# An exact bf16 gather of the sample rows, and the last four experts written outside the loop

## What is computed

```
def moe(xf, w_router, b_router, w1, b1, w2, b2):        # N = 264 tokens, w1[e] 1024x2048, w2[e] 1024x1024
    logits = xf @ w_router + b_router
    top_v, top_e = lax.top_k(logits, TOP_K)             # TOP_K = 4 of 32
    gates = jax.nn.softmax(top_v, axis=-1)
    ...
    def run_block(args):
        e, toks, g = args
        xb = xf[toks]                                   # the gather
        h = xb @ w1[e] + b1[e]
        glu = jnp.minimum(h[:, ::2], SWIGLU_LIMIT)
        lin = jnp.clip(h[:, 1::2], -SWIGLU_LIMIT, SWIGLU_LIMIT)
        a = glu * jax.nn.sigmoid(SWIGLU_ALPHA * glu) * (lin + 1)
        return (a @ w2[e] + b2[e]) * g[:, None]
```

## Time and profile before

| | us |
|---|---|
| median of 3 runs | 1114.68 |
| lowest and highest of them | 1113.35, 1115.1 |
| the profiled execution, its own time | 1113.78 |
| span of the profiled execution | 1112.0 |
| PE busy | 1096.1 |
| DVE busy | 409.0 |
| ACT busy | 165.3 |
| POOL busy | 78.7 |
| bytes moved | 440.43 MB, mean 396 GB/s |

### The profile page before, as it was taken

One profiled execution on the slowest core, in us unless ns is written; L12 is line 12 of the kernel. 1 busy time (PEld: TensorE's weight loads), 2 busy tenths in 40 slices (PEclk: granted clock), 3 DMA queues, 4 the chain that ended last, 5 costly groups with the idle time before them and its releaser, 6 DMA issues.

```text
span 1112.0 us, 14748 instructions
## 1 busy us (share of the span) xinstructions
PE 1096.1 (99%) x5674; PEld 423.5 (38%) x5674; DVE 409.0 (37%) x881; ACT 165.3 (15%) x310; POOL 78.7 (7%) x103
## 2 busy tenths in 40 slices
PE   8999999999999999999999999999999999999998
PEld 6886433333333333333333333333333333332344
DVE  1737763333333333333333333333333333323255
ACT  1622330001000100010001000100001000100043
POOL 0847410000000000000000000000000000000000
PEclk9999999999999999999999999999999999999999
DMA  9988889999999999999999999999999999999971
GB/s 315 266 314 336 255 336 421 426 427 427 430 427 430 427 430 427 428 429 427 429 429 428 429 428 428 427 431 427 428 429 428 429 428 428 427 430 428 428 282 39
DMA packets 48723, 440.43 MB, mean 396 GB/s; under 512 B 10513, under 2 KB 13837, under 8 KB 23766
## 3 DMA queue, kind: packets, MB, share of 16 engines
q1 hardware_dynamic: 47657, 437.43, 94.9%
q0 software_dynamic: 896, 2.66, 0.7%
q10 hardware_dynamic: 148, 0.07, 0.0%
HBM read 436.61 MB, written 3.77 MB: 396 GB/s over the span
## 4 chain that ended last, share of the span: by engine, by line
PE 81%; DMA 11%; SPq 5%; DVE 2%; POOL 1%; issue 0%; ACT 0%; DVEq 0%; POOLq 0%
PE bank L904 36%; PE bank L946 18%; DMA ring<-in_w_mlp 9%; PE bank L843 7%; PE bank L865 5%; PE bank L1022 3%; PE bank L708 2%; PE bank L878 2%; PE bank L928 2%; SPq L356 1%; PE bank L891 1%; POOL ring L1912 1%; PE bank L935 1%; PE bank L871 1%; PE bank L538 1%; DMA q_row<-srow 1%
## 5 line engine op out<-in xcount | busy, mean ns | idle before, releaser
L904 PE MATMUL bank<-ring,proj 128*64 128x512 f32 x2048 | 466.0, 597 | 4.5 <-DMA ring<-in_w_mlp 4.5
L1429 DVE SCALAR_TENSOR_TENSOR xT<-bank,proj,xT 128x512 f32<-128x512 f32 x128 | 90.2, 747 | 440.9 <-PE bank L865 439.6
L904 PEld LDWEIGHTS bank<-ring,proj 128*64 128x64 f32 x2048 | 135.5, 136 | 288.2 <-issue 247.4
L946 PE MATMUL bank<-ring,wpool 128*64 128x512 f32 x1024 | 225.1, 592 | 0.0
L946 PEld LDWEIGHTS bank<-ring,wpool 128*64 128x64 f32 x1024 | 71.2, 137 | 129.9 <-issue 129.0
L1777 ACT ACTIVATE proj<-proj 128x256 f32<-128x256 f32 x64 | 26.7, 416 | 546.5 <-DVE proj L1458 546.5
L843 PE MATMUL bank<-xreg,proj 128*64 128x512 f32 (+1 forms) x396 | 95.4, 599 | 0.1
L538 PE MATMUL bank<-xT,ring 128*128 128x264 f32 x320 | 73.9, 388 | 1.7 <-DMA ring<-in_w_in 1.7
L865 PE MATMUL bank<-mixT 64*128 64x512 f32 x264 | 74.5, 641 | 0.5 <-ACT mixT L1785 0.5
L538 PEld LDWEIGHTS bank<-xT,ring 128*128 128x128 f32 x320 | 60.0, 190 | 13.4 <-issue 3.4
L1785 ACT COPY mixT<-bank 128x512 f32<-128x512 f32 x32 | 18.7, 585 | 232.3 <-PE bank L946 232.3
(11 more groups left out here) (334 smaller groups left out, 624.7 us busy)
## 6 DMA issues: line engine op xcount, KB each, us to landing
ring<-in_w_mlp SPq DMA_DIRECT2D x192, 2048.0 KB, 23.5
ring<-in_w_in SPq DMA_DIRECT2D x10, 1024.0 KB, 13.6
ring<-in_w_out SPq DMA_DIRECT2D x4, 1024.0 KB, 8.3
ring<-in_w_ple_gate SPq DMA_DIRECT2D x4, 1024.0 KB, 28.0
xreg<-in_x_prompt SPq DMA_DIRECT2D x4, 512.0 KB, 4.3
ring<-q_row SPq DMA_DIRECT2D x1, 2048.0 KB, 6.9
ring<-k_row SPq DMA_DIRECT2D x1, 2048.0 KB, 6.7
out<-ring POOLq DMA_DIRECT2D x1, 2048.0 KB, 17.6
```

Of the source, the lines that this page charges most:

```text
L904: last = pe.matmul(bank[q][BLOCK * t:BLOCK * (t + 1), :], xgT[:, k % 4, k // 4, :], ring[:, s, col:col + 512], start=False, stop=(k == KD ...
L946: last = pe.matmul(bank[4][BLOCK * h:BLOCK * (h + 1), :], aT[:, m, BLOCK * t:BLOCK * (t + 1)], w[:, k % 2, 512 * h:512 * h + 512], start=F ...
L1429: ins = STT(total[:, c, s], ins_bank[h][:, :], gate_table[:, c, bass.ds(n, 1)], total[:, c, s], ALU.mult, ALU.add)
```

## The change

Four things are changed together.

The samples' 8 token rows are split into three bf16 parts whose sum is exactly the f32 row: `part_high` is the row rounded to bf16, `part_mid` the rounded rest, and the last part the rest of that. The parts stand in partitions 0, 32 and 64 of a cleared tile (`sample_parts`), the samples' places are copied to the same partitions, and inside the loop the gather's third chunk is one bf16 matmul over 96 rows for each half in place of an f32 matmul over 8. The very first gather (before the loop) stays f32. The split is made before the loop: three casts or copies of 8x1024 and one more copy of the kind on ACT, two copies of the places, two subtractions of 8x1024 on POOL ahead of its two small DMAs, and a clearing of a 128x512 tile on DVE, for which SP's second load of the samples now waits. The wait of the first expert's gather, and of DVE's first one-hot in the loop, take in these steps.

The last four experts stand outside the loop on PE, DVE, ACT and SP. The last of them makes no one-hot, no gather and no transposes of gathered rows.

The last expert's pairs 6, 7 and 10, 11 are issued as single units of 1 MB with rows of 8 KB per partition, and PE waits for each unit by itself (`landed`).

Some semaphores are merged (`ident_in` into `x_in0`, `sn_ready` into `srow_ready`) or dropped (`num_ps`).

```diff
+SINGLES = (6, 10)
...
+        sample_parts = xtok[0:3 * 32, 2, :].bitcast(BF16)[:, 0:D]
+        part_high = sig.rearrange("p q f -> p (q f)")[0:SAMPLES, :].bitcast(BF16)
+        part_mid = act_out[0:SAMPLES, :].bitcast(BF16)
...
+            sp.wait_ge(sem("rest_cleared"), 1)
             sp.dma_start(xtok[0:SAMPLES, 2, :], x_sample[:, 0, :]).then_inc(sem("x_again"), 16)
...
-            def load_body(e, done):
+            def load_body(e, done, closing=False):
                 for n in range(0, UNITS * STEP, 2):
+                    j, u = divmod(n, UNITS)
+                    single = closing and j == STEP - 1 and u in SINGLES
                     sp.wait_ge(sem("units_used"), done + (n - SLOTS + 2))
-                    load_pair(e + n // UNITS, n // UNITS, n % UNITS)
+                    if single:
+                        for a in range(2):
+                            s = slot_of(n + a)
+                            sp.dma_start(ring[:, s, :], unit_weights(e + j, u + a)).then_inc(sem(f"slot{s}"), 16)
+                    else:
+                        load_pair(e + j, j, u)
...
                 for c, (_, m) in enumerate(CHUNKS):
                     for h in range(2):
-                        last = pe.matmul(bank[2][BLOCK * h:BLOCK * (h + 1), :], onehot[0:m, c, 0:BLOCK],
-                                         xtok[0:m, c, 512 * h:512 * h + 512], start=(c == 0), stop=(c == 2))
+                        if c < 2 or n is None:
+                            where, rows_ = onehot[0:m, c, 0:BLOCK], xtok[0:m, c, 512 * h:512 * h + 512]
+                        else:
+                            where, rows_ = onehot16, sample_parts[:, 512 * h:512 * h + 512]
+                        last = pe.matmul(bank[2][BLOCK * h:BLOCK * (h + 1), :], where, rows_, start=(c == 0), stop=(c == 2))
...
-                pe.wait_ge(sem("onehot_ready"), n * 2 + 4)
-                gather(n + 1)
-                pe.wait_ge(sem("hotT_done"), n + 1)
-                spread_places((j + 1) % 2)
+                if not final_one:
+                    if j == 0:
+                        pe.wait_ge(sem("sample_moved"), 11)
+                    pe.wait_ge(sem("onehot_ready"), n * 3 + 5)
+                    gather(n + 1)
+                    pe.wait_ge(sem("hotT_done"), n + 1)
+                    spread_places((j + 1) % 2)
...
-            with pe.Fori(0, npass * EXPERTS, STEP) as n:
+            with pe.Fori(0, npass * EXPERTS - STEP, STEP) as n:
                 for j in range(STEP):
                     expert(n + j, j)
+            for j in range(STEP):
+                expert(npass * EXPERTS - STEP + j, j, True)
...
             dve.wait_ge(sem("mem_ps"), 2)
+            dve.memset(xtok[:, 2, 0:D // 2], 0.0).then_inc(sem("rest_cleared"), 1)
...
+            act.wait_ge(sem("ple_ps"), 3)
+            act.copy(part_high, xtok[0:SAMPLES, 2, :]).then_inc(sem("part_cast"), 1)
+            for q in range(1, 3):
+                act.copy(pos_table[32 * q:32 * q + SAMPLES, 2, :], pos_table[0:SAMPLES, 2, :])\
+                   .then_inc(sem("sample_moved"), 1)
+            act.wait_ge(sem("part_rest"), 1)
+            act.copy(part_mid, xtok[0:SAMPLES, 2, :]).then_inc(sem("part_cast"), 1)
...
+            pool.tensor_tensor(rows_, rows_, part_high, ALU.subtract).then_inc(sem("part_rest"), 1)
+            pool.wait_ge(sem("part_cast"), 2)
+            pool.tensor_tensor(sample_parts[64:64 + SAMPLES, :], rows_, part_mid, ALU.subtract).then_inc(sem("part_rest"), 1)
```

More of the change, by code:

```diff
@@ L465, in _ @@
                 with sp.Fori(1, npass) as b:
-                    with sp.Fori(0, bodies) as i:
+                    load_body(last, b * (EXPERTS * UNITS) - STEP * UNITS)
+                    with sp.Fori(0, bodies - 1) as i:
                         load_body(i * STEP, b * (EXPERTS * UNITS) + i * (STEP * UNITS))
@@ L471, in _ @@
             used = npass * (EXPERTS * UNITS)
+            load_body(last, used - STEP * UNITS, True)
             def wait_slot(s):
@@ L879, in turn_gathered, with landed, expert @@
                 last.then_inc(sem("xgT_ps"), 1)
-            def expert(n, j):
+            def landed(u, i4, closing):
+                s = slot_of(u)
+                if closing and u // UNITS == STEP - 1 and (u % UNITS) // 2 * 2 in SINGLES:
+                    seen = landings(u) if u % 2 == 0 else 1
+                    pe.wait_ge(sem(f"slot{s}"), i4 * 12 + 16 * (before[s] + seen) if u % 2 == 0 else 16 * (before[s] + 1))
+                elif u % 2 == 0:
+                    pe.wait_ge(sem(f"slot{s}"), i4 * 12 + 16 * (before[s] + landings(u)))
+            def expert(n, j, closing=False):
                 i4 = n - j
+                final_one = closing and j == STEP - 1
                 pe.wait_ge(sem("xgT_done"), n + 1)
@@ L895, in expert @@
                     s = slot_of(u)
-                    if k % 2 == 0:
-                        pe.wait_ge(sem(f"slot{s}"), i4 * 12 + 16 * (before[s] + landings(u)))
+                    landed(u, i4, closing)
                     if k == 5:
@@ L940, in expert @@
                     s = slot_of(u)
-                    if k % 4 == 0:
-                        pe.wait_ge(sem(f"slot{s}"), i4 * 12 + 16 * (before[s] + landings(u)))
+                    if k % 2 == 0:
+                        landed(u, i4, closing)
                     w = ring[:, s, :].rearrange("p (a f) -> p a f", a=2)
@@ L952, in _ @@
             pe.wait_ge(sem("onehot_ready"), 1)
-            gather(0)
+            gather(None)
             turn_places()
@@ L1511, in _ @@
             dve.wait_ge(sem("gates_table"), 1)
-            with dve.Fori(0, npass * EXPERTS, STEP) as n:
+            with dve.Fori(0, npass * EXPERTS - STEP, STEP) as n:
                 for j in range(STEP):
                     expert(n + j, j)
+            for j in range(STEP):
+                expert(npass * EXPERTS - STEP + j, j, j == STEP - 1)
             done = npass * (3 * EXPERTS)
@@ L1567, in _ @@
             normalise(1, 1)
[L1568 removed]
+            dve.wait_ge(sem("sample_moved"), 15)
             for half in range(2):
```

83 lines of the change are left out of this document (55 added, 28 removed).

## The result

The changed kernel is slower: 1116.77 us in the median of 15 runs (1115.27 to 1119.46), against 1114.8 us for the kernel before (15 runs, 1113.35 to 1115.42). The ratio is 1.0021, 95% interval 1.0014 to 1.0028, so +1.6 to +3.1 us. The forecast was 1113.5. The profiled execution took 1115.27 us with a span of 1113.5, against 1113.78 and 1112.0.

A forecast was written before the change was run, and what follows sets the result against it. The prediction took the weights' DMA stream (428 GB/s) as the bound. All parts were 0 except -1.18 us in the last expert: 1113.78 to 1112.6 profiled, 1113.5 us from the median of 1114.68; range 1110.6 to 1116.9.

The forecast's parts named there:

- The bound: Whole loop: PE is 99% busy, yet the landing of weights at 428 GB/s comes last for the last six experts.
- The bf16 gather: Gather in 31 experts: 2.72 to 2.03 us, 21 us of PE work, hidden by DVE's activation and DMA waits; value 0.
- The split before the loop: ACT and POOL chain before the loop ends at 167.3, first sigmoid some 0.7 us late, covered by the queue; value 0.
- POOL's two small DMAs at zero: Before the loop: POOL's two DMAs come some 10 us later but are needed only at the end; value 0.
- The last four experts outside: End of the loop: the same instructions in the same order, written outside the loop; value 0.
- The last expert, -1.18: Last expert: w2 can begin at about 1058.64 against 1059.82, and everything behind hangs on PE's end; -1.18 us.
- the singles' -0.84: Last expert: unit 6 loaded singly removes PE's stall before pair 6, 7; unit 7 ends at 1054.49, 0.84 us earlier.
- The turn's -0.34: Last expert, rest of the -1.18: without the gather, w2 waits for DVE's activation, ending 1057.30, and ACT's copy.
- A: Rival, all experts: PE is the limit, so the gather's saving of 21 us is real, 1093; chance 0.03.
- B: Rival, tail: gains all the last unit's landing allows, w2 ends at 1063.2, -3.5 us, 1111.2; chance 0.12.
- C: Rival, expert 0: split and DVE-POOL conflict delay PE 5.9 us, stream runs dry 3.2 us, 1116.7; chance 0.12.
- D: Rival, loop's start: something unlisted moves it a few us either way, paid in full; chance 0.08, half each side.

The follow-up runs named there:

- e9: Kernel before with the bf16 gather, all experts in the loop, samples cut to one bf16 part, no POOL subtractions; ratio 1.0009.
- e7: Kernel before with only the last four experts moved outside the loop; f32 gather, pairs and last gather kept; ratio 1.0011.
- e1: Changed kernel plus six unused f32 matmuls filling PE's idle time in the last expert; 1115.94 us, ratio 1.0006 to the kernel before.
- e4: Kernel before with the last four experts outside the loop and the last expert's singles; f32 gather kept, also in the last expert; ratio 1.0003.
- e2: Kernel before with the last four experts outside the loop and no gather in the last; f32 gather, pairs, no split; ratio 1.0026.
- e14: Kernel before with 128 instructions that do nothing at the head of TensorE's program, same work; ratio 1.0003.
- e6: Changed kernel with six unused f32 matmuls in the last expert and POOL's two small loads issued by SP at about 100 us; ratio 1.0011 to the kernel before.
- e5: Kernel before with POOL's two small loads issued by SP at about 100 us instead; ratio 1.0012.

## Why the prediction was wrong, point by point

**The bound.** Right. The stream decides; PE's 26 us went into waiting. The first stall came earlier (846.93 us), as foreseen.

**The bf16 gather.** Right in size (2.03 us were worked out), and in value as far as PE and the bytes go: e9, which has it, has moved as much as the kernel before by I + 800. PE in the first expert of the changed kernel; from 167.65 to 169.68 it is 2.03, and the wait is longer here than the 0.7 us of later experts, since the sigmoid is late:

```profile
167.65 1.89 PE L870 MATMUL bank<-xreg,proj 128*64 128x512 f32 x8
169.36 0.39 PE L870 MATMUL bank<-xreg,onehot 96*64 96x512 bf16 x2
169.68 0.28 PE L883 MATMUL bank<-place_parts,sel 64*128 64x264 bf16 x1
171.37 0.66 PE L965 MATMUL bank<-cst,proj 128*128 128x128 f32 x4 [1.40 <-DVE proj L1511]
```

**The split before the loop.** The chain on ACT and POOL came out close. In the changed kernel:

```profile
159.86 2.13 POOL L2028 TENSOR_TENSOR xreg<-xreg,proj 8x1024 f32<-8x1024 f32 x1 [4.09 <-ACT proj L1854]
...
165.30 1.04 ACT L1863 COPY xreg<-proj 8x1024 bf16<-8x1024 bf16 x1 [1.16 <-POOL xreg L2030]
167.30 1.28 ACT L1828 ACT_TABLE_LOAD   x1 [0.96 <-ACT xreg L1863]
168.59 0.42 ACT L1828 ACTIVATE proj<-proj 128x256 f32<-128x256 f32 x1
```

It ends at 166.3 (forecast 167.3) and the sigmoid is at 168.59 (forecast near 168.6); POOL's subtraction takes 2.13 us where 2.6 was scaled from another shape. The wrong step is the sentence that set POOL's two small DMAs at zero because they are needed late. They stand behind the subtractions, so they left the DMA gap and fell into the full stream: +0.8 us at the next landing, and 1.0 us of bytes missing by I + 800. When a result is needed doesn't say what its transfer costs the others.

**The last four experts outside, "0".** Wrong: +0.9 us in e7 (0.5 by the pair of expert 30, and 0.5 in the last expert). The instructions are the same, but they are new code, and its fetches are the difference that the traces show. In the changed kernel no stall is left in front of the singles, so a second half doesn't show.

**The last expert, -1.18.** The start of w2 was worked out well: the singles' -0.84 measured -0.92. The turn's -0.34 measured -0.05, but 0.17 of it was never there, since 1059.82 is the chain's start of w2 and the timeline has 1059.65; against that the forecast is -1.01 and the measurement -0.97. Once the gather is gone, the last w2 hangs on the activation and on ACT's copy, with PE waiting 2.85 and 0.40 us. And that wait, which the working itself contained ("the activation takes its place"), was taken as free. It cost 1.4 us of clock. This is the step that turned the sign.

**The sum.** Behind I the changed kernel's stream is 1.38 us late (mean of the two profiles of before, 867.30), the singles and the dropped turn give 0.97 back, so w2 starts 0.41 late; the clock adds 1.44. That is 1.85, and the span ends 1.9 later behind I. The measured ratio says 1.6 to 3.1. Of the stream's 1.38, 0.8 is there at the fourth load, 0.2 comes between the stalls at 905 and 935 us (perhaps new code, though e1 has none of it), and 0.4 in the loop's first turns, at no single place. By the bytes missing at I + 800, 1.0 of it is the whole stream's.

**The rivals.** A (a faster PE pays) is refuted. B didn't come. C gave nearly the right time (1116.7), and it is why the range reached as far as 1116.9. That is luck, since its mechanism was the wrong one: DVE was not held by POOL (its additions beside the subtractions took 1.41 us for two, as before), and PE's w2 in expert 0 was 0.6 us late where C needed over 2.7. By the Trainium skill's rule that was weighed there (SBUF — State Buffer, "SBUF: two separate sides") each meeting could have cost a subtraction; for these instructions no run here shows it. D was too vague to be tested; its truth is that I did not move, but what follows it did. Against the other rule weighed there (the same page, "The DMA setup-cost knee"), two more transfers at the end of the queue cost nothing measurable (e4 with them ends at I + 957.2, e7 without them at 958.3).

## What to carry to other kernels

Where an engine's work is taken away and it then only waits for another, look at what follows the wait: if it is PE and a long row of matmuls is next, the idle time can cost more than the work did, and cheap filler may be the better kernel. On a kernel bound by one unbroken stream, small transfers beside the stream are paid by it (0.7 us for two here) and a fresh stretch of code can be, so place small loads in its gaps, and build a padded copy of the kernel (same work, code moved) before believing a difference below 0.1%. Count from the first load of the stream, not from the span's start: that reading repeated within 0.13 us here where times spread by 2 to 4. Ask at a late landing whether the bytes are late or one engine's share. And take both ends of a difference from one view of the profile.

## What the runs showed of the hardware

- Idle times of 2.85 and 0.40 us with 1.0 us of work between them brought PE to a granted clock of 0.50 for about 3 us (after); 3.22 and 0.42 us with the same work between them did so too (e2); with filler and waits of 0.29 and 0.41 us it stayed at 1.00 (e1).
- A load spread over the DMA engines lands with its last share: with equal bytes moved (341.09 and 341.11 MB) and fifteen of sixteen semaphore updates level, one late share made every later load of e14 land 0.9 us later. It began where a code packet of 0.02 MB was fetched; at other such packets nothing happened.
- Two loads of 4 KB took 0.7 us from a full stream (e1 against e6, by the bytes), and taking them out of the gap ahead of it gained nothing (e5).
- The spread between runs of one kernel goes with the clock: some 100 runs of the kernel before, made beside the experiments, have a median of 1113.9 us where the mean granted clock is 1.000, 1115.2 at 0.998 and 1116.4 at 0.996. In the profiles it falls early on, and that moves the loop's start. The stretch from 40 to 60 us in the kernel before, and in its second profile, where I is 1.19 us later:

```profile
40.00:60.00 20.00, 20.00 (x91) 16.66 (x89) 12.93 (x22) 12.44 (x15) 14.71 (x21) 1.00 0.91 247
```

```profile
40.00:60.00 20.00, 20.00 (x84) 16.29 (x82) 11.29 (x19) 11.97 (x14) 14.45 (x22) 0.91 0.90 231
```
